# First layer's gate units: one matmul of 512 columns for rounded weights on both halves of the activations, bank halves added on VectorE

## What is computed

```python
h = rms_norm(x, mix_norm[l])
(u_a, q_b, f_b, i_b, og_b, cx_c, v_c, o_c, ig_c, fg_c, gates) = jnp.split(h @ w_in[l], splits, axis=-1)
y_a, y_b, y_c = s5_mixer(u_a, ...), hgrn2_mixer(q_b, f_b, i_b, og_b, ...), mlstm_mixer(cx_c, v_c, o_c, ig_c, fg_c, ...)
g_a, g_b, g_c = (gates[..., :D_MODEL], gates[..., D_MODEL:2 * D_MODEL], gates[..., 2 * D_MODEL:])
merged = (jax.nn.sigmoid(g_a) * (y_a @ wb[:r_a]) + jax.nn.sigmoid(g_b) * (y_b @ wb[r_a:r_b])
          + jax.nn.sigmoid(g_c) * (y_c @ wb[r_b:]))
```

## Time and profile before

| | us |
|---|---|
| median of 3 runs | 2983.12 |
| lowest, highest | 2980.38, 2985.36 |
| span of the profiled execution | 2978.0 |
| TensorE matmuls busy | 2946.2 (99%) |
| TensorE weight loads busy | 2630.0 (88%) |
| VectorE busy | 2051.0 (69%) |
| ScalarE busy | 1311.7 (44%) |

### The profile page before, as it was taken

The page is one execution under the profiler, slowest core; times in us unless marked ns, Lnnn a source line. Parts: engine busy times, 40 slices in busy tenths (PEclk is TensorE's granted clock), DMA queues, the critical chain, the costliest instruction groups (busy, mean ns, idle before and its releaser), DMA issues.

```text
span 2978.0 us, 47097 instructions
## 1 busy us (share of the span) xinstructions
PE 2946.2 (99%) x18616; PEld 2630.0 (88%) x18616; DVE 2051.0 (69%) x2624; ACT 1311.7 (44%) x1418; POOL 70.0 (2%) x72
## 2 busy tenths in 40 slices
PE   8999999999999999999999999999999999999999
PEld 8898898999988888888888888876998888888888
DVE  6675787977788888885557776636666666666444
ACT  5354423444444444444444354425445444444333
POOL 0000000000001000000000000000000000000000
PEclk9999999999999999999999999999999999999999
DMA  6553334555555555555555544531555555555555
GB/s 230 184 183 134 114 120 149 168 173 198 186 196 193 189 196 194 190 182 190 193 195 198 195 172 168 186 122 43 184 198 186 195 197 188 193 197 177 194 193 184
DMA packets 87359, 530.39 MB, mean 178 GB/s; under 512 B 9952, under 2 KB 10336, under 8 KB 41184
## 3 DMA queue, kind: packets, MB, share of 16 engines
q1 hardware_dynamic: 87264, 529.07, 50.7%
HBM read 526.94 MB, written 2.10 MB: 178 GB/s over the span
## 4 chain that ended last, share of the span: by engine, by line
PE 96%; DVE 2%; ACT 1%; DMA 0%; issue 0%; SPq 0%; DVEq 0%; ACTq 0%
PE bank L576 74%; PE late L576 22%; DVE arena L1687 1%; DVE w_low L1687 0%; DVE half_low L1687 0%; DVE arena L1684 0%; ACT w_high L1203 0%; PE late L1144 0%; DVE arena L1989 0%; DMA ring<-in_w_gates 0%; DMA xT<-in_xT 0%; DVE acts_both L1687 0%; DVE arena L2045 0%; DVE arena L2016 0%; DVE xrs L1734 0%
## 5 line engine op out<-in xcount | busy, mean ns | idle before, releaser
L1687 DVE TENSOR_TENSOR w_low<-ring,w_high 128x2048 fp32r<-128x2048 f32 (+1 forms) x480 | 1014.3, 2113 | 384.1 <-ACT w_high L1203 380.2
L1203 ACT ACTIVATE w_high<-ring 128x2048 fp32r<-128x2048 f32 (+1 forms) x480 | 849.5, 1771 | 636.0 <-DMA ring<-in_w_down 223.0
L576 PE MATMUL bank<-up_early,w_high 128*128 128x512 f32 x1408 | 487.8, 389 | 0.0
L576 PE MATMUL bank<-up_late,w_high 128*128 128x512 f32 x1408 | 487.3, 389 | 0.0
L576 PE MATMUL late<-acts_both,w_high 128*128 128x512 f32 x1408 | 479.0, 389 | 0.3 <-DVE w_low L1687 0.3
L576 PE MATMUL bank<-up_early,w_low 128*128 128x256 f32 x1408 | 388.6, 276 | 0.0
L576 PE MATMUL late<-acts_both,w_low 128*128 128x256 f32 x1408 | 388.6, 276 | 0.0
L576 PE MATMUL bank<-up_late,w_low 128*128 128x256 f32 x1408 | 388.6, 276 | 0.0
L576 PEld LDWEIGHTS bank<-up_early,w_high 128*128 128x128 f32 x1408 | 264.5, 188 | 55.2
L576 PEld LDWEIGHTS late<-acts_both,w_high 128*128 128x128 f32 x1408 | 264.3, 188 | 55.1 <-DVE w_low L1687 0.6
L576 PEld LDWEIGHTS bank<-up_late,w_high 128*128 128x128 f32 x1408 | 264.0, 188 | 54.7
(11 more groups left out here) (311 smaller groups left out, 4946.2 us busy)
## 6 DMA issues: line engine op xcount, KB each, us to landing
ring<-in_w_up SPq DMA_DIRECT2D x176, 1024.0 KB, 4.7
ring<-in_w_down SPq DMA_DIRECT2D x128, 704.0 KB, 4.0
ring<-in_w_in SPq DMA_DIRECT2D x66, 1024.0 KB, 4.7
ring<-in_w_mix SPq DMA_DIRECT2D x62, 1024.0 KB, 4.8
ring<-in_w_gates SPq DMA_DIRECT2D x96, 512.0 KB, 3.7
ring<-in_w_branch SPq DMA_DIRECT2D x16, 1024.0 KB, 4.7
ring<-in_w_out SPq DMA_DIRECT2D x16, 1024.0 KB, 4.8
ring<-in_w_o SPq DMA_DIRECT2D x16, 1024.0 KB, 4.8
```

The costliest lines, as they stand in the source:

```text
L576: return nc.tensor.matmul(o, lhsT, rhs, start=first, stop=last)
L1203: A(w_high[:, s, 0:cols], ring[:, s, 0:cols], ACT.Copy).then_inc(rounded[s], 1)
L1687: return V.tensor_tensor(o, a, b, op)
```

## The change

For the rounded weights the two matmuls of 256 columns become one of 512, whose moving operand is the pair (h_low, h_high) and whose output is the whole bank; w_high x h_high then stands in the second half of the bank, the rest in the first. ScalarE no longer writes the sigmoid from the bank: it copies the first half to the gate's arena tile (gate_copied). VectorE adds the second half to it (sum_gate) and gives the bank back. ScalarE writes the sigmoid in place one gate later (gate_sigmoid). sum_gate(c-2) stands in lower_gate of gate c between its two halves; the last two stand behind the last lower_gate. The two operands stay where they were; a strided alias (h_both) spans hT and the arena.

```diff
-        h_high, h_low = alias("h_high", arena_base, [P, KT, T], 46), alias("h_low", hT_base, [P, KT, T])
+        h_apart = (arena_base - hT_base) // 4 + 46 * T
+        h_both = alias("h_both", hT_base, [P, 2 * h_apart])[:].rearrange("p (a d) -> p a d", a=2)[:, :, 0:KT * T]
+        h_low, h_high = (h_both[:, a].rearrange("p (k t) -> p k t", t=T) for a in range(2))
...
@@ TensorE, gate
-                        mm(bank[at][:, 0], half_high[:, s, c], h_high[:, k], k == 0, False)
-                        mm(bank[at][:, 0], half_high[:, s, c], h_low[:, k], False, False)
+                        mm(bank[at][:], half_high[:, s, c], h_both[:, :, k * T:(k + 1) * T], k == 0, False)
...
@@ ScalarE, gate(c)
-                at = gate_tile(c)
-                A(arena[:, at * T:(at + 1) * T], bank[s][:, 0], ACT.Sigmoid).then_inc(drained[s], 1)
+                A(gate_at(c), bank[s][:, 0], ACT.Copy).then_inc(gate_copied, 1)
+                if c:
+                    gate_sigmoid(c - 1)
+                waiting[c] = (s, halves.drained[s].value())
+
+            waiting = {}
+
+            def gate_sigmoid(c):
+                s, there = waiting[c]
+                act.wait_ge(drained[s], there)
+                A(gate_at(c), gate_at(c), ACT.Sigmoid)
...
             gate(GATES - 1)
+            gate_sigmoid(GATES - 1)
...
@@ VectorE
+            gates = [0]
+
+            def sum_gate(c):
+
+                at = (2 * c + 1) % RING
+                dve.wait_ge(gate_copied, c + 1)
+                tt(gate_at(c), bank[at][:, 1], gate_at(c), ADD).then_inc(drained[at], 1)
+
             def lower_gate():
                 for half in range(2):
                     s, _, _, _, _ = half_units.next(False, split=True)
+                    if half and gates[0] >= AHEAD:
+                        sum_gate(gates[0] - AHEAD)
                     dve.wait_ge(half_rounded[s], half_units.rounded[s].value())
                     tt(half_low[:, s], half_raw[:, s], half_high[:, s].bitcast(F32), SUB).then_inc(half_lowered[s], 1)
+                gates[0] += 1
...
+            for c in range(GATES - AHEAD, GATES):
+                sum_gate(c)
             for m, at in enumerate((Q0, O0)):
                 dve.wait_ge(y_rounded, m + 1)
```

More of the change, by code:

```diff
@@ L375, in build @@
         half_copied = sem("ff_low_half_copied")
+        gate_copied = sem("gate_low_half_copied")
         x_normed, gains_made = sem("x_normalised"), sem("mix2_gains_made")
@@ L396, in v, with gate_at @@
             return vec[0:rows_, c:c + 1]
+        def gate_at(c):
+            at = gate_tile(c)
+            return arena[:, at * T:(at + 1) * T]
         def all_tiles(sq, n):
```

## The result

| | us |
|---|---|
| before, median of 15 runs | 2980.53 (2974.51 to 2985.81) |
| after, median of 15 runs | 2989.84 (2984.07 to 2993.64) |
| ratio | 1.0033, 95% interval 1.0024 to 1.0041 |
| span of the profiled execution after | 2986.1 (before 2978.0) |

The change makes the kernel slower, by 0.33%, some 10 us; the forecast was no change. The forecast range, 2973 to 2991 us, was laid around a median of 2983.12 for the kernel before, so it stood for a change of -10 to +8 us. 15 runs put that median at 2980.53, and against that the 9 to 10 us lie above the range's edge, though 2989.84 itself is inside. One thing about the metric: the profiled execution of the changed kernel had a device time of 2987.91 us over a span of 2986.1, so only 1.8 us lie around a span. The 5.1 us that I put there were mostly the difference between one run and the median.

What follows compares the result with a forecast made beforehand. TensorE looked full but VectorE had the least room: TensorE loses 15.4 us of work, VectorE gains 17. The stretches summed to -0.4 us against a median of 2983.12, giving 2983 us; likeliest 2978 to 2988, 8 in 10 2973 to 2991.

Steps and rivals of the forecast that it cites:

- to gate 19: 448 to 477 us, gates 16 to 18: chain on TensorE, so the joined matmuls gain 0.9 us.
- the S5 rounds: 509 to 642 us, three rounds of seven gates: VectorE's 43.7 plus a 0.9 wait gives 44.7 a round, -0.3 each.
- What one joined matmul saves: All 48 gates on TensorE: 0.34 instead of 0.36 us a k-tile, 5.44 a gate, 15.4 us in all.
- Gate 8: 382.2 to 387.8 us: whole gate starts behind lowering and sum, with 1.8 us for the clock; ends 389.6, cumulated +1.8.
- The levels: 390 to 441 us: the bound moves to VectorE, TensorE catches up the 1.8 us over six periods, 0.32 each.
- the catching up of 4.5 us: Within the sum: gain from the joined matmuls, 4.5 us, gone if they save nothing.
- 477 to 509: VectorE late: gates 20 and 21 wait for lowering and sum, four sums 1.4 us, half taken up by a wait; +0.7.
- 642 to 663: Gates 45 to 47 beside a nearly idle VectorE, gate 47 still waiting for the lowering: -0.4 us.
- The tail: After gate 47: the last sum waits for ScalarE's copy, branches start 2.8 us later, 1.55 of idling hidden; net +1.4.
- Rival 2: Late gate starts cost the clock: six more falls give 2994 us, below four stays within the measurement; chance 0.15.
- Rival 1: TensorE's gain arrives because VectorE's waits give way: up to 15.4 us, 2968, or 2975 with half; chance 0.18.
- Rival 3: The joined matmul saves nothing, or nearly so, as its operand's halves lie apart: near 2989 us; chance 0.07.

Runs made afterwards that it cites:

- e5: Changed kernel with the gates taking turns on three banks instead of two: 2975.61 us, 0.9995 of the time before the change.
- e1: Changed kernel with the joined matmul kept, but VectorE's sum, ScalarE's copy and the later sigmoid taken out: 2970.59 us, 0.9977 of before.
- e7: Changed kernel with the joined matmul reading two neighbouring tiles of the high activations (wrong numbers in the gates): one run, 2993.63 us.
- e8: Changed kernel with TensorE waiting for lowered weights first in each half, then alternating matmuls of 512 and 256 columns: one run, 2991.3 us.
- e9: Changed kernel with three banks for the gates and the joined matmul split into two of 256 columns, sums kept: 2984.38 us, 1.0024 of before.
- e10: Changed kernel with three banks for the gates and gate 47 copied before the first branch weights are rounded: 2974.76 us, 0.9989 of before.
- e3: Changed kernel with the sum of gate c-2 moved ahead of the first half's lowering of gate c: 2980.03 us, 1.0009 of before.
- e6: Changed kernel with ScalarE writing each gate's sigmoid two gates later instead of one: 2985.85 us, 1.0034 of before.
- e4: Changed kernel with ScalarE copying gate 47 before it rounds the first branch weights: 2985.23 us, 1.0029 of before.
- e2: Changed kernel with the joined matmul undone into two of 256 columns, sums left in: 2989.82 us, 1.0048 of before.
- e11: As e10, with the sum also moved ahead of the first lowering: 2976.47 us, 0.9996 of before.

## Why the prediction was wrong

**The bound, as I read it, was right and too weak.** VectorE is the engine without room, and TensorE's 15.4 us do not arrive. But I put the loss into VectorE's amount of work (43.7 of 44.7 us in a round), and the runs show that the amount fits: e5 has 43.11 us of VectorE in a round of 43.81. The moved wait was what counted, and I had it only as single events of one or two us. By stretch the sum missed 7.9 us at the out projection (-0.4 against +7.5):

| stretch | forecast | measured |
|---|---|---|
| up to the end of gate 8 | +1.8 | +3.0 |
| the levels, to the end of their matmuls | -2.1 | -1.1 |
| to gate 19 | -0.9 | -0.5 |
| to S5 output 1 | +0.7 | +1.2 |
| S5 outputs 1 to 4 | -0.9 | +2.5 |
| to the GLU | -0.4 | +0.2 |
| tail | +1.4 | +2.1 |

The step that failed is the fifth: the S5 rounds, with 3.4 of the 7.9 us.

**What one joined matmul saves** (first term): forecast 0.34 a tile and 5.44 a gate from the earlier trace rows; measured 5.59. Half of the 0.32 a gate was there, 0.16, so 7.7 us in all instead of 15.4; e1 gives 6.5 of them at the out projection. I carried the spacing from one place of the kernel to another, and neither the distance nor the order explains the difference (e7, e8). The forecast was 20 ns a tile, measured are 10. The estimate from the Trainium skill ("TensorE: Matmul & The Clock Gate", Back-to-back issue gap), 2.6 ns a tile and 2 us in all, was nearly as far off on the other side.

**Gate 8**: forecast +1.8, measured +3.0. The mechanism and the place were right, and the start at 382.35 as well, that by luck: gates 0 to 3 gave 0.6 us instead of 1.3, but TensorE was 0.56 us early before gate 0 (its chain has that start at 300.73, before at 301.29), which no edit explains. The size of the clock term failed: I carried over the 1.8 us of a gate that had done a third of its work before the pause. Now the pause was 4.37 instead of 2.19 us, the granted clock was 0.50 through 384 to 388, and the gate took 8.51, which is 2.9 over 5.59. The price of a pause is not a constant that one row gives, and its length alone doesn't give it either: for TensorE's pause of 2.0 us in this place, the kernel before and e1 paid 1.6 to 1.8 us, e5, e9 and e10 nothing.

**The levels**: "TensorE catches up 1.8". With 0.16 instead of 0.32 a period it caught up 1.1 (+3.0 to +1.9). The mis-sized first term again; the levels' period is 8.27 on TensorE. In all, the catching up of 4.5 us in the sum counted that term at twice its size, which is 2.3 of the 7.9 us.

**477 to 509**: forecast +0.7. The place was right (gates 20 and 21 wait 0.92 and 1.66 us for the sum), and from +1.4 at gate 19 the shift grew by 1.2 to 2.6.

**The S5 rounds**: this is the step that failed. Forecast -0.3 a round, measured +0.2 and +0.7, then +1.6 into output 4. I added up VectorE's work and one wait of 0.9 (43.7 and 0.9 are 44.6, where I wrote 44.7, and how 0.9 follows from 4.9 us is not shown), as if VectorE alone set the pace and TensorE's wait at the start of a gate cost nothing on top. VectorE's rows in the round from 556.89 look different in kind: of 45.67 us it is idle for 2.6. The rows of the changed kernel show the ring:

```profile
547.90 1.23 DVE L1703 TENSOR_TENSOR half_low<-ring,half_high 128x1024 fp32r<-128x1024 f32 x1 [0.51 <-ACT half_high L1403]
549.04 0.42 DVE L1703 TENSOR_TENSOR arena<-bank,arena 128x256 f32<-128x256 f32 x1
550.45 1.22 DVE L1703 TENSOR_TENSOR half_low<-ring,half_high 128x1024 fp32r<-128x1024 f32 x1 [0.99 <-ACT half_high L1403]
```

The chain of waits in this round shows one turn of it: a gate's end, the load into its slot, the rounding, VectorE's work, the sum, and the start of a later gate:

```profile
540.00 25.99 PE bank L583 x160
566.01 4.14 DMA ring<-in_w_gates
570.18 1.07 ACT half_high L1403
...
577.05 1.22 DVE half_low L1703
578.27 0.35 DVE arena L1703
578.66 5.85 PE bank L583 x32
```

A gate that starts late ends late, so its slot is loaded late, rounded late, and VectorE waits for it two gates on, in front of its own steps, which make a later gate start late. With slots for two gates and two banks the delay comes round again. In this round VectorE waits 0.32, 0.75 and 1.06 us for rounded weights and TensorE 1.51 for the sum ahead of the gate at 578.66, and these waits alternate instead of overlapping. e3 (gate may start one lowering earlier, -4.6 us) and e5 (no such wait, -10.9 us) show that it is this start; e6 shows that ScalarE's wait is not part of it. That the loads pass the delay on is read from the rows; no kernel with more slots was run.

**642 to 663**: forecast -0.4, measured +0.2: gates of 5.59, and gate 47 waited 0.49 for the sum.

**The tail**: forecast +1.4 (2.8 less 1.55 is 1.25), measured +2.1. The mechanism was there as told: DVE waited 6.65 us for the copy of gate 47, and the branches began 2.15 us behind the GLU's end (forecast 2.8). e4 took it back by ordering two instructions of ScalarE. What I had not counted is the clock behind the pause. The chain of waits of the changed kernel, and its stretches with the granted clock (third number from the end):

```profile
677.99 3.91 PE bank L583 x18
...
684.01 2.12 PE bank L583 x18
```

```profile
676.00:680.00 4.00, 2.01 (x10) 2.01 (x11) 3.79 (x3) 4.00 (x6) 0.00 (x0) 0.79 0.75 268
680.00:684.00 4.00, 4.00 (x30) 4.00 (x29) 4.00 (x3) 3.00 (x3) 0.00 (x0) 0.78 0.62 260
```

The first 18 branch matmuls take 3.91 us where 18 take 2.12, at a clock of 0.79 and 0.78 between its two levels: 1.8 us that no term of mine held. It does reach the sum. The second unit's weights were lowered in time:

```profile
679.28 2.29 DVE L1703 TENSOR_TENSOR w_low<-ring,w_high 128x2048 fp32r<-128x2048 f32 x1 [0.21 <-ACT w_high L1209]
```

They were done at 681.57, and without the fall of the clock TensorE would have come to that unit at 682.2; it came at 684.01. So the late start by itself was worth some 0.3 us of the +2.1, since the 1.55 us that TensorE idled there before the change are saved, and the clock 1.8. That forecast and measurement lie as near as 0.7 here is in part luck. Nor does the pause's length give this price: behind a pause of 2.90 us in the same place e3 took 3.92 us for the 18 matmuls, behind one of 2.87 us e5 took 2.36.

**The rivals.** Rival 2 was nearest: the late start of gates was the cause. But it was priced by the clock, and among the late starts in the changed kernel the clock fell only at gate 8 and behind the pause ahead of the branches; PEld's waits of 1.3 to 1.8 us left it at 1.00. (It also fell at 308 to 316, as it had at 316 to 324 before the change, at the same cost.) In e7 it fell to 0.57 behind such a wait of 2.03 us ahead of 623.3, where e4, behind 2.02 us, kept 1.00; that it stayed up is no rule. Rival 1 would have come true by nearly half without the sums (e1, 0.23% faster), and less with them and three banks (e10, 0.11%). Rival 3 had the right doubt about the spacing, at half its size.

## What to carry to other kernels

When a change moves the instruction that gives a buffer back behind another step, ask first who can no longer start early; a few hundred nanoseconds of work on the fullest engine may fit where 1 us of lost overlap per turn doesn't, because it travels round the ring of slots. A third buffer lay free here and was worth more than all the matmul time saved. Take the spacing of matmuls from the stage that is changed. Price a pause of TensorE as a range that starts at nothing, unless several traces show the same: one execution's row may be chance.

## What the hardware showed unexpectedly

The same pause of TensorE, in the same place, behind the same work, brings a fall of the clock in one profile and none in another. At gate 8 a pause of 2.0 us left the granted clock at 0.74 in the kernel before and in e1, and at 1.00 in e5, e9 and e10. Ahead of S5 output 1 a pause of 2.19 us left it at 0.70 in e5 and at 1.00 in e10. Ahead of the branches 2.90 us left it at 0.70 in e3, and 2.87 us at 1.00 in e5. Each of these falls cost 1.6 to 1.8 us. That is nearly the 2.2 us of e4's whole effect, so a shift of the marks of 1.6 us is not by itself an edit's doing. Why it falls or not is open.

TensorE's spacing also changes by steps without any pause or fall of the clock, in stages that no kernel touched. The out projection in the chain of waits, in the changed kernel and in e4:

```profile
768.81 96.61 PE bank L583 x556
```

```profile
766.61 93.89 PE bank L583 x556
```

The same 556 matmuls take 2.7 us more (0.35 us for a pair of 512 and 256 columns instead of 0.34, at a granted clock of 1.00), in the changed kernel and in e7; before, and in all the others, they take 93.9. The first down projection took 232.2 us before, in the changed kernel and in e1, e2, e4 to e6, e8, e10 and e11, and 239.0 in e3, e7 and e9. I have one profile of each kernel. The times of the runs speak for the execution and not the kernel: the profiled run of e3, one with 239.0, took 2986.68 us, 6.7 above the kernel's median, and six of e1's nine runs lie at 2969.6 to 2970.8 and two at 2976.4 to 2976.6. That isn't proof, as no second profile was taken. Between the two profiles of before and after these steps nearly cancel: the out projection adds 2.7 us, a later one 0.9, and between 1965 and 2082 us the kernel before lost 3.0 more than the changed one, at a mean granted clock of 0.97. So the spans differ by 8.1 us, and the rest of the 9.8 is the spread of executions. In e9 the 239.0 makes the profile longer than its marks say; whether most of its runs had it isn't known. The cause, and whether the 0.230 us of the joined matmuls is the same thing, stays open.
